# Two more buffers for the streamed expert weights of a two-block transformer kernel, and an expert loop written over pairs of quads

## The reference

```python
def hier_moe(t, w_rg, b_rg, w_re, b_re, w_gate, w_up, w_down):
    g_logits = (t @ w_rg + b_rg).astype(jnp.float32)
    ...
    y = jnp.zeros_like(t)
    for e in range(N_EXPERTS):                               # 32
        he = jax.nn.silu(t @ w_gate[e]) * (t @ w_up[e])      # 1024 -> 512
        y = y + combine[:, e:e + 1] * (he @ w_down[e])       # 512 -> 1024
    return y
```

## Time and profile before

| | us |
|---|---|
| median of 3 runs | 1710.09 (1709.39 to 1710.91) |
| the profiled execution, device time | 1711.51 |
| the profiled execution, span of the trace | 1709.7 |
| mean granted clock of TensorE, share of full speed | 0.916 |
| TensorE busy | 1367.1 (80%) |
| VectorE / ScalarE / GpSimd busy | 784.2 / 448.1 / 326.3 |
| moved by transfers | 582.89 MB |

### The profile page before, as it was taken

The page is one execution under the profiler, slowest core; times in us unless marked ns, Lnnn a source line. Parts: engine busy times, 40 slices in busy tenths (PEclk is TensorE's granted clock), DMA queues, the critical chain, the costliest instruction groups (busy, mean ns, idle before and its releaser), DMA issues.

```text
span 1709.7 us, 18915 instructions
## 1 busy us (share of the span) xinstructions
PE 1367.1 (80%) x6976; PEld 783.7 (46%) x6976; DVE 784.2 (46%) x1906; ACT 448.1 (26%) x1211; POOL 326.3 (19%) x272
## 2 busy tenths in 40 slices
PE   6999998996878787779988767799967675666665
PEld 3467886785444443435544322487722221222122
DVE  2102764327778786798878885506400010000003
ACT  1111214303434343355444343215100100010010
POOL 0000000002444344444555455002000000000000
PEclk8999999998989899989999999899987878888888
DMA  9556327837999999999999999552299999999994
GB/s 394 240 196 259 143 99 307 333 123 283 421 422 421 423 418 422 420 392 370 403 422 420 421 421 421 210 191 99 99 399 428 429 429 428 428 428 429 429 429 187
DMA packets 60121, 582.89 MB, mean 341 GB/s; under 512 B 6672, under 2 KB 7056, under 8 KB 7952
## 3 DMA queue, kind: packets, MB, share of 16 engines
q1 hardware_dynamic: 21600, 306.66, 43.4%
q0 software_dynamic: 36864, 268.45, 38.2%
q10 hardware_dynamic: 1584, 6.83, 1.0%
HBM read 580.87 MB, written 1.05 MB: 340 GB/s over the span
## 4 chain that ended last, share of the span: by engine, by line
PE 41%; DMA 40%; DVE 11%; ACT 4%; issue 3%; POOL 1%; SPq 0%; DVEq 0%; ACTq 0%
PE ps L955 38%; DMA big<-peer_uv,big 19%; DMA big<-w_stream 11%; DMA slab<-w_stream 10%; DVE big L2010 4%; PE ps L1201 1%; POOL big L578 1%; PE ps L1209 1%; ACT big L823 1%; ACT big L819 1%; DVE stat L1874 1%; DVE big L2021 0%; PE ps L1112 0%; DVE big L1958 0%; ACT big L815 0%
## 5 line engine op out<-in xcount | busy, mean ns | idle before, releaser
L955 PE MATMUL ps<-big 128*128 128x512 f32 (+3 forms) x1946 | 609.0, 588 | 211.9 <-ACT big L823 139.0
L955 PEld LDWEIGHTS ps<-big 128*128 128x128 f32 (+1 forms) x1946 | 256.1, 181 | 537.7 <-ACT big L823 231.9
L578 POOL DMA_INDIRECT big<-peer_uv,big x256 | 315.3, 1232 | 756.0 <-DVE big L1994 407.9
L2010 DVE CUSTOM_DVE_ANT_0 big<-big 128x1024 f32<-128x1024 f32 x256 | 310.7, 1225 | 123.8 <-DMA big<-peer_uv,big 120.1
L955 PE MATMUL ps<-slab,big 128*32 128x512 f32 x1024 | 153.6, 738 | 70.7 <-DMA slab<-w_stream 67.4
L955 PE MATMUL ps<-hT,slab 128*128 128x128 f32 (+1 forms) x1216 | 182.2, 308 | 0.0
L955 PEld LDWEIGHTS ps<-hT,slab 128*128 128x128 f32 x1216 | 168.3, 191 | 19.7 <-issue 10.4
L815 ACT ACTIVATE big<-big 128x1 f32<-128x1 f32 x256 | 51.6, 201 | 348.9 <-DVE big L2010 348.2
L955 PEld LDWEIGHTS ps<-slab,big 128*32 128x32 f32 x1024 | 32.4, 123 | 174.6 <-DMA slab<-w_stream 97.2
L2214 DVE TENSOR_TENSOR big<-big,ps 128x512 f32<-128x512 f32 x8 | 5.5, 688 | 220.1 <-PE ps L955 220.1
L955 PE MATMUL ps<-slab,hT 128*128 128x256 f32 (+2 forms) x304 | 91.5, 458 | 7.9 <-issue 4.7
(11 more groups left out here) (324 smaller groups left out, 1177.8 us busy)
## 6 DMA issues: line engine op xcount, KB each, us to landing
slab<-w_stream SPq DMA_DIRECT2D x113, 2048.0 KB, 19.5
big<-w_stream SPq DMA_DIRECT2D x32, 2048.0 KB, 23.2
big<-peer_uv,big POOLq DMA_INDIRECT x256, 11.6
big<-rpb ACTq DMA_DIRECT2D x1, 1536.0 KB, 11.3
cst<-consts ACTq DMA_DIRECT2D x1, 1312.0 KB, 16.9
xT<-x_t SPq DMA_DIRECT2D x1, 1024.0 KB, 6.5
hcT<-ctx_t SPq DMA_DIRECT2D x1, 1024.0 KB, 25.6
scratch<-sub_keys ACTq DMA_DIRECT2D x1, 1024.0 KB, 11.0
```

Of the source, the lines that this page charges most:

```text
L578: nc.gpsimd.indirect_dma_start(out=uv[b], out_offset=None, in_=peer_uv, in_offset=bass.IndirectOffsetOnAxis(ap=idxu[:, s:s + 1], axis=0)). ...
L955: ins = nc.tensor.matmul(*a, **kw)
L2010: V.tensor_tensor_reduce(out=u, in0=u, in1=xtok, scale=1.0, scalar=0.0, op0=ALU.mult, op1=ALU.add, accum_out=dots[:, s:s + 1]).then_inc(do ...
```

## The change

The expert ring gets eight slots in place of six. The two new ones are `scratch` (all of it) and `big` 14592 to 18688, where the second attention's keys and biases lay. SP starts E6 and E7 into them as soon as the last head's product is made and the last logits are scaled; E1 is started ahead of these two waits. From E8 on, slab Ei waits for E(i-8), and SP's loop has 12 turns of eight transfers.

For this, what lay in these two places and is still needed later is moved: the router's weights to `small`, the vector `shifted` that is computed from them to `sc0`, and the squares of normalizations 7 and 8 to `hT`.

Since 12 slabs don't divide by eight slots but 24 do, TensorE's loop runs over 4 pairs of quads, with the body written out twice (`odd` 0 and 1). The matrix products are the same, in number and order. The loops of VectorE and ScalarE over 8 quads stay.

```diff
-EXTRA = 2
+EXTRA = 4
 MOE_SLOTS = SLOTS + EXTRA
...
-        wr = at(big, 18176, KD * (NG + NE))
-        extra = [at(big, 10496, SLAB), at(big, 6400, SLAB)]
+        wr = at(small, 0, KD * (NG + NE))
+        extra = [at(big, 10496, SLAB), at(big, 6400, SLAB), at(scratch, 0, SLAB), at(big, 14592, SLAB)]
...
-        shifted = at(small, 0, KD * (NG + NE))
+        shifted = at(sc0, 0, KD * (NG + NE))
...
+            if i >= 7:
+                return hT[:, k * T:(k + 1) * T]
...
             extra_load(1, S_MOE + SLOTS + 1)
-            for n in range(S_MOE + 1, S_MOE + SLOTS):
+            load(S_MOE + 1, (S_MOE + 1) % SLOTS, S_MOE + 1 - SLOTS + 1)
+            sp.wait_ge(head_filled, 2 * UNITS)
+            extra_load(2, S_MOE + SLOTS + 2)
+            sp.wait_ge(scaled, 2 * UNITS)
+            extra_load(3, S_MOE + SLOTS + 3)
+            for n in range(S_MOE + 2, S_MOE + SLOTS):
                 load(n, n % SLOTS, n - SLOTS + 1)
...
-                with pe.Fori(0, QUADS) as q:
-                    t = r * QUADS + q
-                    ring = r * (QUADS * Q_SLABS // MOE_SLOTS) + q * (Q_SLABS // MOE_SLOTS)
+                with pe.Fori(0, QUADS // 2) as h:
+                  for odd in range(2):
+                    t = r * QUADS + h * 2 + odd
+                    ring = r * (QUADS * Q_SLABS // MOE_SLOTS) + h * (2 * Q_SLABS // MOE_SLOTS)
...
-                            w = expert_weights(4 * b + s, ring).rearrange("p (e k n) -> p e k n", e=QUAD, k=2)
+                            w = expert_weights(odd * Q_SLABS + 4 * b + s, ring).rearrange("p (e k n) -> p e k n", e=QUAD, k=2)
...
-                        w = expert_weights(8 + f, ring).rearrange("p (e n) -> p e n", e=QUAD)
+                        w = expert_weights(odd * Q_SLABS + 8 + f, ring).rearrange("p (e n) -> p e n", e=QUAD)
```

## The result

| | before | changed | 
|---|---|---|
| median, runs of the same session | 1710.68 us (5 runs, 1709.39 to 1711.40) | 1700.77 us (5 runs, 1699.21 to 1704.37) |
| ratio, 95% interval | | 0.9947 (0.9936 to 0.9958) |
| profiled execution, device time / span | 1711.51 / 1709.7 us | 1704.37 / 1702.6 us |
| TensorE busy | 1367.1 us | 1366.0 us |

The change makes the kernel faster by 9.9 us in the medians; 0.53% by the ratio, with 0.42 to 0.64% as its interval. The predicted median was 1700.3.

What follows compares the result with a forecast made beforehand. Transfers were taken to bound the expert stage, whose end follows the continuous stream's start and the slabs already in. Terms -9.8 + 0.1 = -9.7 us from 1710.09 gave about 1700.3 us, range 1698.0 to 1703.5.

Steps and rivals of the forecast that it cites:

- The price of a slab: Expert stream: each slab costs 4.912 us, so two slabs in early gain 9.8 us.
- Room for the pair: Idle transfers before the stream: E6 and E7 land at about 1200.7, 4 us before E2's start; costs nothing.
- SP's new waits: SP's queue after attention: two added waits hold up only E2 and E3, which start later anyway; cost nothing.
- Products beside the transfers: Output projection running beside E6 and E7: 0 to +0.16 us, taken as 0.1.
- Moved tiles: Squares, router's weights and `shifted` in new places: taken at 0; even 10% on the squares would be 0.3 us.
- The loop over pairs: TensorE's expert loop: seven returns become three, body doubled; 0 on the path, upper bound 50 us a pair.
- the reserve: TensorE's waiting for slabs in the expert stage, 25 us a quad, 50 a pair, able to hide stops.
- Rival C: Expert stage: loop returns over 50 us each make TensorE set the end; no change, 1710 us; chance 0.03.
- The stream's rate: Continuous expert stream: keeps 428 GB/s with the deeper queue, which buys no rate.
- Rival B: All 88 stream transfers lose rate from longer queue and instruction fetches; at 5.07 us a slab 1714.2; chance 0.03.
- The tail: From E95's first product to the end: unchanged at 24.0 us, clock may make it -1.4 to +2.2.
- TensorE's waits for slabs: Weight loads' waits in the expert stage: sink from 203 to about 193 us.

Runs made afterwards that it cites:

- E6: Not a run: an expert weight slab, started at 1240.82 us before the change and at 1188.11 in the changed kernel.
- E7: Not a run: the expert weight slab after E6, started at 1188.48 us in the changed kernel.
- E8: Not a run: the expert weight slab that begins the continuous stream in the changed kernel, at 1240.79 us.
- E95: Not a run: the last expert weight slab; its first product came at 1685.68 us before and 1675.76 in the changed kernel.
- E3: Not a run: an expert weight slab loaded ahead of the continuous stream, started at 1221.07 us before the change.
- E2: Not a run: an expert weight slab loaded ahead of the continuous stream, started at 1204.64 us before and 1204.61 in the changed kernel.
- the filled gaps: Changed kernel plus two unread products behind each of the first three down slabs of a quad; 1699.09 us, ratio 0.9940.
- all three executions with the copy: Changed kernel with E8 also loaded ahead and copied by GpSimd: 1695.25 us, again 1694.62; with two unread products behind three down slabs per quad 1695.95.

## Why the prediction was right

The likeliest case came, and each of its steps can be read in the trace.

- **The price of a slab.** Predicted 4.912 us, so 9.8 for two. E95's first product came 9.92 us earlier (1685.68 to 1675.76). That it fell within 0.2 us of the forecast moment, 1675.9, is partly luck: the two profiled executions reached the stream at the same moment (1240.82 and 1240.79), where others differed by up to 3 us. Of the 88 slabs of the stream, each took (1675.76 - 1240.79) / 88 = 4.94 us including the first one's latency; 444.86 / 90 = 4.94 before. With none, one and two slabs early it was 444.6, 439.8 and 435.0 us from the stream's start to E95.
- **Room for the pair.** Predicted starts 1188.2 and 1188.6, measured 1188.11 and 1188.48; predicted 260 GB/s in the window to 1204.5, measured 262. The trial with both behind E3 shows that the room was larger than was needed.
- **SP's new waits.** Predicted 0. E2 starts at 1204.61 (1204.64 before) and E8 at 1240.79.
- **Products beside the transfers.** 0.1 us was taken; the output projection's first 64 products took 14.08 us both times, so it is 0.
- **Moved tiles.** Taken at 0. The kernel without the head start has them all in their new places, and its ratio is 1.0002.
- **The loop over pairs.** Predicted 0 on the path, with the reserve as the only upper bound. Measured 1710.44 against 1710.31 with this part alone, and no gap at a return. Rival C falls. The Trainium skill (Runtime: NRT & Kernel Launch, "Instruction fetch mechanics") has it both ways, two pages of 16 KiB and a larger memory of 2048 instructions for TensorE; that no return stopped and that only two packets more were fetched agrees with the larger memory and not with the two pages. How large it is, no run here shows.
- **The stream's rate.** Rival B falls: 428 GB/s with 32.1 us from start to landing, where it was 22.5 at the same rate. That is 6.5 slabs on their way in place of 4.6, at 4.94 us a slab in both.

```profile
slab<-w_stream SPq DMA_DIRECT2D x44, 2048.0 KB, 32.1
```

- **The tail.** Taken at 24.0 us with -1.4 and +2.2 as bounds. The profiled run had 26.8, 2.8 more, outside: E95's products took 3.64 us and the sums 6.15, where 1.92 and 3.72 are the shortest seen, together 4.15 us. The upper bound left out that E95's products could be slower too: 3.31 us was read as their time at the low clock, but the granted clock over them was 0.57, and at 0.50 they take 3.64 (still less than a slab's 4.9, so nothing else hangs on it). Six of the ten experiments had 22.6 or 22.7, the others 24.0 to 26.1. This is where the single execution misled: the kernel before was profiled with a tail in the middle.

One statement was wrong: TensorE's waits for slabs were to sink from 203 us to about 193. They are 107.3 + 70.3 + 24.6 = 202.2 us:

```profile
PEld ps L962 <- DMA slab<-w_stream: 107.3, 33, 3.9
PEld ps L962 <- DMA big<-w_stream: 70.3, 23, 3.9
PEld ps L962 <- DMA scratch<-w_stream: 24.6, 7, 3.9
```

The step that failed counted the whole gain as time in which TensorE waits. The stage is 10 us shorter, but TensorE was also busy 4.8 us less in it (289.51 in place of 294.34, with as many products and a clock of 0.83 in place of 0.82), so only some 5 of the 10 us came off its idle time. That time has pieces which this count of the weight loads' waits doesn't hold: the waits of the products themselves for slabs sank by 6.5 us, from 133.3 to 126.8. The loop over pairs on six slots has 200.4 us of the weight loads' waits with nothing gained, and the filled gaps have 159.0 with the same stream as the change. In this stage, bound by transfers, the clock shifts time between work and waiting and leaves the end where it is; a count of waits doesn't measure the gain.

## What to carry to other kernels

Where a long stream of weights keeps the transfer engines busy all the time, as here at 428 GB/s, its end is fixed by when it begins and how many bytes are left then: count the rest of the transfer engines ahead of it and the buffers that die there, and price each slab that fits by its own transfer time. More slots as such brought nothing once the stream ran: the eight slots without the head start measured 1.0002. A slab for which there is no slot in the ring can still be loaded ahead into any dead memory and be copied into place by an idle engine, if the copy ends before the slab is asked for.

## What was not expected of the hardware

GpSimd copied 128 x 2048 float32 between two tiles in 1.89 us, so a whole slab in 3.8 us, less than the 4.9 us of its transfer from memory (times of GpSimd are rough in a profile, but all three executions with the copy have 1.88 and 1.89). TensorE worked beside both halves, the transfers only beside the second: they moved nothing during the first and 164 GB/s during the second, 1.88 us. What a copy takes next to the stream at its full rate is not shown. And the tail behind the last slab, the same instructions every time, took between 22.6 and 26.8 us in the profiled executions, by the clock that two groups of 16 products met: 0.50 and 0.59 in the longest tail, 1.00 and 1.00 in the short ones. That is 4 us or 0.25% of the whole kernel, more than the difference between some of the kernels compared here.
